# Half-width chunks for the first memory keys and the convolution inputs, and one low part on another engine

## The reference

```python
h = rms_norm(x, pre_mix_g);  z = h @ w_in
za, zb, zc = z[..., :512], z[..., 512:2048], z[..., 2048:2560]
ya = spatial_gating(gelu(za), ...)        # layer norm of half of gelu(za)
q, k, v = split(zb, 3);  yb = moba_attention(q, k, v)
yc = conformer_conv(zc, ...)              # a * sigmoid(g), then a causal depthwise conv of 31 taps
x = x + rms_norm(concat(ya, yb, yc) @ w_out)
m = rms_norm(mem, mem_g);  k, v = split(m @ w_kv, 2)    # memory keys and values, 4 heads of 256
x = x + rms_norm(cross_attention(rms_norm(x), k, v) @ w_o)
x = x + rms_norm(square(relu(rms_norm(x) @ w_ff1)) @ w_ff2)
```

## Time and profile before

| | |
|---|---|
| Median of 3 runs | 748.2 us (748.14 to 748.3) |
| The profiled execution | 748.35 us, of which the instructions span 746.6 us |
| TensorE busy | 738.8 us (99%) |
| VectorE busy | 527.6 us (71%) |
| ScalarE busy | 405.6 us (54%) |
| GpSimd busy | 49.6 us (7%) |
| Mean granted TensorE clock | 0.998 of full |

### The profile page before, as it was taken

One profiled execution on the slowest core, in us unless ns is written; L12 is line 12 of the kernel. 1 busy time (PEld: TensorE's weight loads), 2 busy tenths in 40 slices (PEclk: granted clock), 3 DMA queues, 4 the chain that ended last, 5 costly groups with the idle time before them and its releaser, 6 DMA issues.

```text
span 746.6 us, 10142 instructions
## 1 busy us (share of the span) xinstructions
PE 738.8 (99%) x4152; PEld 641.8 (86%) x4152; DVE 527.6 (71%) x618; ACT 405.6 (54%) x515; POOL 49.6 (7%) x71
## 2 busy tenths in 40 slices
PE   9999999999999999999999999999999999999996
PEld 9988888889988888888899898788987888888885
DVE  6788946885766666666779997886758655566564
ACT  6578378544545545444653685674647443454442
POOL 0200002120000000000230200030003000000000
PEclk9999999999999999999999999999999999999999
DMA  9866366555565556665476436364165566555531
GB/s 337 281 225 227 136 234 213 172 169 171 172 223 169 170 173 205 205 206 211 157 213 210 158 125 226 112 224 155 47 213 166 161 222 226 173 201 185 166 121 57
DMA packets 77278, 138.40 MB, mean 185 GB/s; under 512 B 3884, under 2 KB 34480, under 8 KB 77104
## 3 DMA queue, kind: packets, MB, share of 16 engines
q1 hardware_dynamic: 75376, 132.69, 52.9%
q10 hardware_dynamic: 1856, 5.06, 2.0%
HBM read 136.69 MB, written 1.05 MB: 184 GB/s over the span
## 4 chain that ended last, share of the span: by engine, by line
PE 96%; DVE 2%; DMA 1%; ACT 1%; issue 0%; SPq 0%; DVEq 0%; ACTq 0%
PE wide L2109 70%; PE bank L2109 24%; PE bank L2238 2%; DMA raw<-in_w_in_dram 1%; DVE low L1350 0%; DVE arena L1613 0%; ACT arena L734 0%; DVE act_hl L1447 0%; ACT act_hl L734 0%; DVE xn L1833 0%; DVE x L1843 0%; DVE arena L1676 0%; DVE hid_l L1679 0%; DVE arena L1674 0%; DVE arena L1670 0%
## 5 line engine op out<-in xcount | busy, mean ns | idle before, releaser
L1350 DVE TENSOR_TENSOR low<-raw,high 128x2048 fp32r<-128x2048 f32 (+1 forms) x118 | 267.0, 2278 | 102.9 <-ACT high L734 99.0
L734 ACT ACTIVATE high<-raw 128x2048 fp32r<-128x2048 f32 (+3 forms) x134 | 234.6, 1770 | 117.2 <-PE wide L2109 92.6
L2109 PE MATMUL wide<-act_hl,high 128*128 128x512 f32 (+1 forms) x1056 | 240.2, 346 | 0.3 <-ACT high L734 0.3
L2109 PEld LDWEIGHTS wide<-act_hl,high 128*128 128x128 f32 x1056 | 183.1, 191 | 24.0 <-issue 0.5
L2109 PE MATMUL wide<-high,act_hl 128*128 128x512 f32 x528 | 170.0, 394 | 0.5 <-DVE act_hl L1447 0.3
L2109 PE MATMUL wide<-act_hl,low 128*128 128x256 f32 x832 | 160.7, 283 | 0.0
L2109 PEld LDWEIGHTS wide<-act_hl,low 128*128 128x128 f32 x832 | 128.1, 191 | 2.7 <-DVE low L1398 0.2
L2109 PEld LDWEIGHTS wide<-high,act_hl 128*128 128x128 f32 x528 | 99.2, 188 | 23.3 <-issue 1.7
L2109 PE MATMUL wide<-low,act_hl 128*128 128x512 f32 x264 | 103.0, 390 | 0.0
L2109 PE MATMUL bank<-high,hid_l 128*128 128x512 f32 x216 | 84.4, 391 | 0.2 <-DVE hid_l L1679 0.2
L734 ACT ACTIVATE arena<-wide 128x512 f32<-128x512 f32 x59 | 33.0, 595 | 94.7 <-PE wide L2109 94.7
(11 more groups left out here) (212 smaller groups left out, 680.7 us busy)
## 6 DMA issues: line engine op xcount, KB each, us to landing
raw<-in_w_ff_dram SPq DMA_DIRECT2D x32, 1024.0 KB, 5.3
raw<-in_w_in_dram SPq DMA_DIRECT2D x27, 1024.0 KB, 5.1
raw<-in_w_ffn_in_dram SPq DMA_DIRECT2D x40, 512.0 KB, 4.9
raw<-in_w_ffn_out_dram SPq DMA_DIRECT2D x11, 1024.0 KB, 6.8
raw<-in_w_xkv_dram SPq DMA_DIRECT2D x8, 1024.0 KB, 5.0
raw<-in_w_o_dram SPq DMA_DIRECT2D x4, 1024.0 KB, 5.0
raw<-in_w_out_dram SPq DMA_DIRECT2D x4, 1024.0 KB, 5.0
raw<-in_w_xq_dram SPq DMA_DIRECT2D x4, 1024.0 KB, 5.0
```

Source lines behind the costliest of these rows:

```text
L734: return act.activation(dst, src, func, **k)
L1350: tt(part(low, g), part(raw, g), f32(part(high, g)), SUB).then_inc(sem.low_by_dve, 1)
L2109: return pe.matmul(dst, lhs, rhs, start=start, stop=stop, skip_group_check=loose)
```

## The change

The plan cuts kv0 and zc into two chunks of 256 columns each, each one group of eight k tiles; zc's second half of columns (the gate g) comes first. TensorE works them in mode "H", for the memory with a new layout in which the high and low parts of the normalised memory lie in one tensor. ScalarE and VectorE add up the PSUM halves (`low_part`, `half_total`), then make the high and low parts of the keys (`kv_high`, `k_mem_low`) and the tanh of the gate. `xq_part` and `xq_sum` are renamed `low_part` and `half_sum` and counted over both uses. `pool_groups` keeps only the second group of v2, and three calls of `ahead_of` leave GpSimd's program.

```diff
@@ plan_weights
-    add_kv(0)
-    for key, c in (("zc", 2048), ("q2", 512), ("k2", 1024), ("za", 0), ("v2", 1536)):
+    for i in range(2):
+        add(("kv", 0, i), w["w_xkv_2"], 0, KD, [(0, i * 256, 256)], 256)
+    for i, c in enumerate((2048 + 256, 2048)):
+        add(("zc", i), w["w_in_2"], 0, KD, [(0, c, 256)], 256)
+    for key, c in (("q2", 512), ("k2", 1024), ("za", 0), ("v2", 1536)):
         add(key, w["w_in_2"], 0, KD, [(0, c, NB)], NB)
@@ tiles
-        hid_h = [sb(f"hid_h{i}", [P, 4, T], F32R) for i in range(2)]
-        hid_l = [sb(f"hid_l{i}", [P, 4, T], F32R) for i in range(2)]
+        hid_hl = sb("hid_hl", [P, 2, 2, 4, T], F32R)
+        hid_h, hid_l = ([hid_hl[:, part_i, i] for i in range(2)] for part_i in range(2))
@@
-        pool_groups = {chunks["q2"][1][0], chunks["v2"][1][0]}
+        pool_groups = {chunks["v2"][1][0]}
@@ GpSimd's program
             block2_masks()
-            ahead_of("q2", "C")
-            ahead_of("k2", "C")
-            ahead_of("za", "T")
             ln_rstd()
             ahead_of("v2", "T")
@@ ScalarE: new functions
+            def low_part(dst):
+                act.wait_ge(sem.w_used, me.used)
+                f(dst, wide_of(me.half(), 1), ACT.Copy).then_inc(sem.low_part, 1)
+            def kv_high(i):
+                k = slice(2 * i, 2 * i + 2)
+                act.wait_ge(sem.half_sum, me.seen("half_sum"))
+                f(k_high[:, k, :], k_mem[:, k, :], ACT.Copy).then_inc(sem.kv_in, 1)
+            def zc_tanh():
+                act.wait_ge(sem.half_sum, me.seen("half_sum"))
+                f(cs, cs, ACT.Tanh, scale=0.5).then_inc(sem.zc_t, 1)
@@ ScalarE's program
-            ahead_of_half(("kv", 0), 0)
+            ahead_of(("kv", 0, 0), "H")
             norm_stat(2)
-            ahead_of_half(("kv", 0), 1)
+            low_part(k_mem[:, 0:2, :])
+            ahead_of(("kv", 0, 1), "H")
             load_block2()
             norm_split(2)
-            kv_in(0)
-            ahead_of("zc", "C")
-            zc_in()
+            low_part(k_mem[:, 2:4, :])
+            kv_high(0)
+            ahead_of(("zc", 0), "H")
+            kv_high(1)
+            low_part(in2(cs))
+            zc_tanh()
+            ahead_of(("zc", 1), "H")
+            low_part(in2(cx))
@@ VectorE: new functions
+            def half_total(dst):
+                dve.wait_ge(sem.low_part, me.seen("low_part"))
+                tt(dst, wide_of(me.half(), 0), dst, ADD).then_inc(sem.half_sum, 1)
+            def k_mem_low(i):
+                k = slice(2 * i, 2 * i + 2)
+                dve.wait_ge(sem.kv_in, i + 1)
+                tt(hid1_h[i][:, :, :], k_mem[:, k, :], f32(k_high[:, k, :]), SUB).then_inc(sem.x_low, 1)
@@ VectorE's zc_in
-                dve.memset(glu[:, :, 0:DW_TAPS - 1], 0.0).then_inc(sem.dve_step, 1)
+                dve.wait_ge(sem.low_part, me.seen("low_part"))
+                tt(in2(cx), wide_of(me.half(), 0), in2(cx), ADD).then_inc(sem.dve_step, 1)
...
-                stt(glu[:, :, DW_TAPS - 1:], in2(cs), 1.0, in2(me.pair()[0][:, :]), ADD, MUL).then_inc(sem.zc_in, 1)
+                stt(glu[:, :, DW_TAPS - 1:], in2(cs), 1.0, in2(cx), ADD, MUL).then_inc(sem.zc_in, 1)
@@ VectorE's program
-            ahead_of_half(("kv", 0), 0)
+            ahead_of(("kv", 0, 0), "H")
+            half_total(k_mem[:, 0:2, :])
             norm_split(2)
-            ahead_of_half(("kv", 0), 1)
-            kv_low(0, me.pair())
-            ahead_of("zc", "C")
+            ahead_of(("kv", 0, 1), "H")
+            half_total(k_mem[:, 2:4, :])
+            k_mem_low(0)
+            ahead_of(("zc", 0), "H")
+            k_mem_low(1)
+            half_total(in2(cs))
+            dve.memset(glu[:, :, 0:DW_TAPS - 1], 0.0).then_inc(sem.dve_step, 1)
+            dve.wait_ge(sem.dve_step, me.step())
+            ahead_of(("zc", 1), "H")
             zc_in()
@@ TensorE's program
-            products(("kv", 0), "C", is_mem=True, at={KD - 1: turn_scaled})
-            products("zc", "C", fresh=True)
-            pe.wait_ge(sem.x_low, 2)
+            products(("kv", 0, 0), "H", is_mem=True)
+            products(("kv", 0, 1), "H", is_mem=True, at={KD - 2: turn_scaled})
+            pe.wait_ge(sem.half_sum, me.seen("half_sum"))
+            products(("zc", 0), "H", fresh=True)
+            pe.wait_ge(sem.half_sum, me.seen("half_sum"))
+            products(("zc", 1), "H")
+            pe.wait_ge(sem.half_sum, me.seen("half_sum"))
             products("q2", "C")
```

More of the change, by code:

```diff
@@ L252, in __init__ @@
         self.xq_in = new("xq_in")
-        self.xq_part = new("xq_part")
-        self.xq_sum = new("xq_sum")
+        self.low_part = new("low_part")
+        self.half_sum = new("half_sum")
         self.y_a = new("y_a")
@@ L464, in split_of, with both_of @@
             return act_hl[:, kt // 2, 0, k], act_hl[:, kt // 2, 1, k]
-        def both_of(kt):
+        def both_of(kt, is_mem=False):
+            if is_mem:
+                return hid_hl[:, :, kt // 4, kt % 4, :]
             return act_hl[:, kt // 2, :, kt % 2 * T:(kt % 2 + 1) * T]
@@ L1017, in xq_part @@
                 act.wait_ge(sem.w_used, me.used)
-                f(x_q[:, i % 2 * 2:i % 2 * 2 + 2, :], wide_of(me.half(), 1), ACT.Copy, scale=1 / 16).then_inc(sem.xq_part, 1)
+                f(x_q[:, i % 2 * 2:i % 2 * 2 + 2, :], wide_of(me.half(), 1), ACT.Copy, scale=1 / 16).then_inc(sem.low_part, 1)
             def hidden1(c):
@@ L1044, in kv_in @@
             def kv_in(c):
-                if c < 2:
-                    k = (k_high, k_mem)[c]
-                    copy_pair(k[:, 0:2, :], k[:, 2:4, :], sem.kv_in)
+                if c == 1:
+                    act.wait_ge(sem.x_low, 2)
+                    copy_pair(k_mem[:, 0:2, :], k_mem[:, 2:4, :], sem.kv_in)
                 else:
@@ L1051, in xq_high @@
             def xq_high(i):
-                act.wait_ge(sem.xq_sum, i + 1)
+                act.wait_ge(sem.half_sum, me.seen("half_sum"))
                 f(hid_h[0][:, 2 * i:2 * i + 2, :], x_q[:, 2 * i:2 * i + 2, :], ACT.Copy).then_inc(sem.x_high, 1)
@@ L1057, in qk2_in @@
                 copy_pair(d[:, 0:2, :], d[:, 2:4, :], sem.qk2_in, (0.125, 1.0)[i])
-            def zc_in():
+            def low_part(dst):
                 act.wait_ge(sem.w_used, me.used)
-                f(cs, me.pair()[1][:, :], ACT.Tanh, scale=0.5).then_inc(sem.zc_t, 1)
+                f(dst, wide_of(me.half(), 1), ACT.Copy).then_inc(sem.low_part, 1)
[4 more added lines that the diff above has]
+            def zc_tanh():
+                act.wait_ge(sem.half_sum, me.seen("half_sum"))
+                f(cs, cs, ACT.Tanh, scale=0.5).then_inc(sem.zc_t, 1)
             def high_of_bank(q, b, done):
@@ L1849, in kv_low @@
                     dve.wait_ge(sem.kv_in, 2 * c + i + 1)
[L1850 to L1853, removed]
+                    tt(v_low[c - 2][:, i, :], b[:, :], f32(v_high[c - 2][:, i, :]), SUB).then_inc(sem.x_low, 1)
             def xq_total(i):
                 d = x_q[:, i % 2 * 2:i % 2 * 2 + 2, :]
-                dve.wait_ge(sem.xq_part, i + 1)
-                stt(d, wide_of(me.half(), 0), 1 / 16, d, MUL, ADD).then_inc(sem.xq_sum if i < 2 else sem.xq_in, 1)
+                dve.wait_ge(sem.low_part, me.seen("low_part"))
+                stt(d, wide_of(me.half(), 0), 1 / 16, d, MUL, ADD).then_inc(sem.half_sum if i < 2 else sem.xq_in, 1)
             def xq_low(i):
@@ L2179, in products @@
                             o = bank[2 * parity + t]
-                            mm(o[:, :], wh[:, j, ch], both_of(kt), s0, False)
+                            mm(o[:, :], wh[:, j, ch], both_of(kt, is_mem), s0, False)
                             ins = mm(o[:, 0:T], wl[:, j, ch], in_h, False, s1)
@@ L2657, in _ @@
             products(("xq", 1), "H")
-            pe.wait_ge(sem.xq_sum, 1)
+            pe.wait_ge(sem.half_sum, me.seen("half_sum"))
             products(("xq", 2), "H")
             x_scores(0)
-            pe.wait_ge(sem.xq_sum, 2)
+            pe.wait_ge(sem.half_sum, me.seen("half_sum"))
             products(("xq", 3), "H")
```

## The result

The changed kernel takes 762.87 us (median of 4 runs, 762.04 to 763.38) against 748.25 us before: a ratio of 1.0194, 95% interval 1.0182 to 1.0206. It is 14.6 us slower. The profiled execution took 762.04 us with a span of 760.3 us, 13.7 us more than before in both.

The account below looks back on a forecast made before the run. TensorE, busy 99% of the span, was taken as the bound. The profiled 748.35 us plus 12.4 for the late low part and 2.3 for the clock gave 763.05, predicted as 763.0 us; range 760.0 to 766.5.

Parts of the forecast that it names:

- GpSimd's order decides: In GpSimd's program, v2's second low part now stands behind `ln_rstd` and waits for the statistics, ending at 443.5.
- Rival 1: v2's second low part is not late; only the products' 0.44 us remain, 747.9 us; chance 0.06.
- 12.4 us late: TensorE begins v2's second group at 443.6 instead of 431.17, after statistics at 437.5 and GpSimd's steps.
- 4.3 us given back at 420: VectorE's six taps at 420.56, blocked 4.3 us by GpSimd's subtraction before, take 2.71 us instead of 7.05.
- Rival 3: VectorE wins nothing back at 420.56, held by something else; statistics 1.8 us late, 766.2 us; chance 0.05.
- 2.3 us for the clock: TensorE's clock falls in the pause before v2's second group; restarting costs 2.3 us, bounds 0 and 3.5.
- Rival 2: TensorE's clock does not fall in the pause, or recovers at once: 760.8 us; chance 0.06.
- 0.44 us of the products, lost in the wait: Four half-width groups save TensorE 0.44 us, but it merely arrives earlier at v2's second group and stands still 12.8 us.
- Nothing behind it: After v2's second group nothing is given back and nothing added; the later load and VectorE's queue are covered.
- Rival 4: New sums stop an engine longer, say ScalarE's wait delaying q2's second group beyond 393.6; perhaps 765 us; chance 0.03.

Follow-up runs that it names:

- e1_order: Changed kernel with one line moved: GpSimd's look-ahead for v2 stands ahead of `ln_rstd` again; 748.03 us against 748.46 for the kernel before, ratio 0.9993.
- e2_pool_only: Kernel before with GpSimd's part of the change alone (`pool_groups` and three look-aheads), chunks still 512 columns wide; 763.44 us, ratio 1.0196.
- e5_chunks_only: Changed kernel with `pool_groups` and GpSimd's program as before, so the half-width chunks alone; 747.85 us against 748.31, ratio 0.9997.
- e4_warm: Changed kernel with 48 unused 512-column matmuls on TensorE between the two groups of v2; 761.07 us, ratio 1.0167.
- e6_stats_later: Changed kernel with VectorE's taps 22 and 23 ahead of the layer norm's statistics instead of behind them; 763.83 us, ratio 1.0208.
- e7_stats_earlier: Changed kernel with VectorE's taps 20 and 21 moved behind the layer norm's statistics; 762.59 us, ratio 1.0192.
- e3_no_pool: Changed kernel with no group on GpSimd, VectorE making v2's second low part too; 748.03 us, ratio 0.9994.

## Why the prediction was right

Predicted 763.0 us, measured 762.87. By its steps:

- *GpSimd's order decides.* Right, and shown from both sides (e1_order, e2_pool_only). Rival 1, that the low part isn't late, fell at once: GpSimd didn't take the ready subtraction ahead of an operation that waited. By the Trainium skill (TensorE: Matmul & The Clock Gate, Architectural detail, the paragraph on engine queue depths), GpSimd is strict FIFO per core; the 59.63 us of idle time ahead of line 686, with a subtraction ready behind it since about 420, agree.
- *12.4 us late.* Measured 11.94 from start to start of the second group, or 12.34 with kv0's start 0.40 us earlier allowed for. The terms: the gate's product ended at 391.64 where I had 392.3; the maxima at 421.79 where I had 422.4; 1.15 us late instead of 1.8. Of these differences 0.40 us is the earlier start; the rest is that each of VectorE's steps overlaps the one before by some 0.08 us, which my sum of durations left out. The statistics came at 437.01 (I had 437.5), GpSimd was done at 443.05 (443.5). What set this point was mistaken, though. I summed VectorE's work and gave ScalarE's last copy 0.1 us; in the trace the copy came last, and it hangs on TensorE's end of v2's first group. In e2_pool_only, where VectorE had 1.59 us to spare, the pause is 12.87 us all the same. That the two ways meet within 0.25 us in the changed kernel is luck.
- *4.3 us given back at 420.* Right, all but the 0.25 us that VectorE then idled: 2.70 us for the six taps, and 7.05, 5.71, 3.94 (e5_chunks_only) or 2.71 us in the others just as GpSimd's operation lay. Rival 3 fell.
- *2.3 us for the clock.* The mechanism was right, the size 0.4 us too large: 1.86 us here, 1.5 in e2_pool_only (6.93 - 5.44). My term came from the kernel's start, where the low stretch was longer: here the lower rate held from 443.11 to about 446.8 (an estimate from the mean of 0.80 granted between 446 and 448), 3.7 us against the 5.3 us that I had read there. Rival 2, no fall, is ruled out by the granted 0.50 and by e4_warm.
- *0.44 us of the products, lost in the wait.* This step was wrong, by too little to show in the total. The groups saved 0.30 us net, as zc's first group waited 0.2 us for the activations, as foreseen. But the wait doesn't swallow it: with TensorE done earlier ScalarE's copy, the statistics and the end of the pause come earlier too. From kv0's start to the start of v2's second group it takes 80.10 us in the changed kernel and 80.40 in e2_pool_only, with full-width chunks; the 0.30 us is there in full.
- *Nothing behind it.* Right: the stretch from kv1 to the end shows no new wait of TensorE. Rival 4 did not happen: q2's second low part was there at 390.3 (388.02 + 2.29), 3 us ahead of TensorE's need at 393.4.

The closeness of the total, 0.1 us, is partly luck: the pause and the clock came out some 0.4 us lower each than predicted, and the median lies 0.8 us above the profiled execution. The changed kernel's runs spread over 1.3 us where the four of before in the same comparison spread over 0.2; but 21 runs of the kernel before spread over 1.4 us in the first experiments, so the pause is not needed to explain that. The group behind the pause took 7.30, 6.93, 7.16 and 7.21 us in four profiles (the changed kernel, e2_pool_only, e6_stats_later, e7_stats_earlier): it varies by 0.4 us, and why is open.

## What to carry to other kernels

When work moves from one engine to another, read the program of the engine that loses it for what else the removed lines did: here a look-ahead that was written for one group carried another, and without it a ready operation stood behind a wait of 59 us on an in-order queue. On a kernel whose bound engine never idles, price such an operation by the end of the wait ahead of it, not by its own duration, and add the clock for any pause of this length. Then ask what that wait itself hangs on: where its end is tied to the stalled engine's own last work, as here, relieving the engine between them buys nothing (e7_stats_earlier).

## What the runs showed of the hardware

GpSimd's 128x2048 subtraction blocks some of VectorE's operations for its whole length and leaves others alone. Blocked: convolution taps (two operands in SBUF, 4.3 us longer for six) and a `TENSOR_SCALAR` of 128x256 with one SBUF operand (4.47 us instead of 0.41). Without GpSimd's subtraction (e3_no_pool) six taps take 2.71 us. Not blocked: in e5_chunks_only GpSimd subtracts from 420.33 to 424.93, and VectorE's scores from PSUM (1.94 us) and maxima (1.81 us) pass at their usual length, while the taps at 423.50 wait:

```profile
420.33 4.60 POOL L596 TENSOR_TENSOR low<-raw,high 128x2048 fp32r<-128x2048 f32 x1 [27.46 <-ACT high L739]
```

```profile
419.80 1.94 DVE L1765 SCALAR_TENSOR_TENSOR arena<-arena,bank 128x384 f32<-128x384 f32 x4
421.77 1.81 DVE L1770 TENSOR_REDUCE neg_max<-arena 128x4 f32<-128x512 f32 x2
423.50 3.94 DVE L1497 SCALAR_TENSOR_TENSOR arena<-arena,vec 128x256 f32<-128x256 f32 x6
```

It goes the other way in small: GpSimd's own three steps took 5.95 us beside VectorE's taps and 5.50 us beside an idle VectorE. That agrees with the shared port pair of the Trainium skill (SBUF — State Buffer, SBUF: two separate sides), where a VectorE operation of two SBUF inputs or in a two-port mode contends with GpSimd's. Whether the `TENSOR_SCALAR` runs in such a mode no row here says.
